# A two-layer state-space and gating kernel: five products a chunk instead of six in most weight tiles

## The reference, cut to what matters

```
def _layer(x, mod, h0, lw, rows):
    shift, scale, gate = jnp.split(mod, 3, axis=-1)
    h = rms_norm(x, norm_w) * (1 + scale[:, None]) + shift[:, None]
    proj = h @ w_in
    xbc_raw, z_m, dt_raw, u_raw, v_raw, z_g, gl_m, gl_g = jnp.split(proj, ...)
    y_m, h_fin = _ssd_branch(xbc_raw, dt_raw, z_m, ...)   # conv of 5 taps, scan in both directions
    y_g = _gmlp_branch(u_raw, v_raw, z_g, ...)
    merged = jax.nn.sigmoid(gl_m) * (y_m @ w_out_m) + jax.nn.sigmoid(gl_g) * (y_g @ w_out_g)
    return x + gate[:, None] * (merged @ w_out), h_fin
```

## Time and profile before

| | |
|---|---|
| median of 3 runs | 1404.17 us (1403.57 to 1405.57) |
| span of the profiled execution, first to last instruction | 1402.5 us |
| TensorE busy | 1389.5 us, 10045 products |
| VectorE busy | 1020.4 us |
| GpSimd busy | 1028.4 us |
| ScalarE busy | 467.2 us |
| HBM read, written | 178.70 MB, 26.02 MB |
| mean granted TensorE clock | 0.997 |

### The profile page before, as it was taken

One profiled execution on the slowest core, in us unless ns is written; L12 is line 12 of the kernel. 1 busy time (PEld: TensorE's weight loads), 2 busy tenths in 40 slices (PEclk: granted clock), 3 DMA queues, 4 the chain that ended last, 5 costly groups with the idle time before them and its releaser, 6 DMA issues.

```text
span 1402.5 us, 26918 instructions
## 1 busy us (share of the span) xinstructions
PE 1389.5 (99%) x10045; PEld 1333.8 (95%) x10045; DVE 1020.4 (73%) x1503; ACT 467.2 (33%) x1040; POOL 1028.4 (73%) x1421
## 2 busy tenths in 40 slices
PE   8999999999999999999999999999999999999997
PEld 6899899999999999999998999999999999999997
DVE  4888679675677688989978766986566776769234
ACT  4432133213766333001242323241266661320122
POOL 3699886596654589998869898757765546979773
PEclk9999999999999999999999999999999999999999
DMA  9262665223766555444334455732346655453222
GB/s 369 91 151 86 184 164 165 68 61 121 186 187 183 170 222 210 149 154 149 110 136 122 106 164 148 179 99 61 106 132 190 192 177 190 149 189 121 76 76 90
DMA packets 197902, 206.31 MB, mean 147 GB/s; under 512 B 76576, under 2 KB 163744, under 8 KB 196640
## 3 DMA queue, kind: packets, MB, share of 16 engines
q1 hardware_dynamic: 115856, 154.61, 35.4%
q10 hardware_dynamic: 81936, 50.16, 12.2%
HBM read 178.70 MB, written 26.02 MB: 146 GB/s over the span
## 4 chain that ended last, share of the span: by engine, by line
PE 98%; DVE 1%; issue 0%; POOL 0%; ACT 0%; DVEq 0%; POOLq 0%; ACTq 0%
PE acc L708 80%; PE X L675 5%; PE acc L675 3%; PE X L947 2%; PE X L927 2%; PE X L963 1%; PE X L988 1%; PE acc L841 1%; PE X L956 1%; PE acc L788 0%; PE X L800 0%; DVE h_pre L1622 0%; DVE xr L2107 0%; DVE p_lo L1577 0%; PE acc L800 0%
## 5 line engine op out<-in xcount | busy, mean ns | idle before, releaser
L609 POOL CAST w_hi<-w_st 128x256 fp32r<-128x256 f32 x696 | 412.7, 607 | 340.8 <-PE acc L708 168.7
L613 POOL TENSOR_TENSOR w_lo<-w_st,w_hi 128x256 fp32r<-128x256 f32 x696 | 644.4, 935 | 0.0
L708 PE MATMUL acc<-h_hi,w_hi 128*128 128x320 f32 x1696 | 402.1, 318 | 0.0
L708 PE MATMUL acc<-h_lo,w_hi 128*128 128x320 f32 x1696 | 386.4, 309 | 0.0
L708 PE MATMUL acc<-h_hi,w_lo 128*128 128x320 f32 x1696 | 386.1, 309 | 0.0
L708 PEld LDWEIGHTS acc<-h_hi,w_hi 128*128 128x128 f32 x1696 | 284.5, 188 | 14.7 <-issue 11.8
L708 PEld LDWEIGHTS acc<-h_hi,w_lo 128*128 128x128 f32 x1696 | 283.5, 188 | 0.0
L708 PEld LDWEIGHTS acc<-h_lo,w_hi 128*128 128x128 f32 x1696 | 283.2, 188 | 0.0
L1788 DVE SCALAR_TENSOR_TENSOR cv<-raw,convw_sb,cv 128x642 f32<-128x642 f32 x128 | 137.1, 1071 | 4.5
L1511 DVE SCALAR_TENSOR_TENSOR ada_acc<-ada_st,sc,ada_acc 128x512 f32<-128x512 f32 x112 | 107.1, 995 | 1.8
L1251 ACT ACTIVATE cvt<-cv 128x642 f32<-128x642 f32 x32 | 23.8, 744 | 162.6 <-DVE cv L1788 162.6
(11 more groups left out here) (266 smaller groups left out, 2320.9 us busy)
## 6 DMA issues: line engine op xcount, KB each, us to landing
w_st<-in_wts SPq DMA_DIRECT2D x174, 512.0 KB, 3.7
cum_bc<-cum_dram ACTq DMA_DIRECT2D x80, 256.0 KB, 4.9
ada_st<-in_wada SPq DMA_DIRECT2D x34, 512.0 KB, 4.5
ex_bc<-ex_dram ACTq DMA_DIRECT2D x64, 128.0 KB, 3.0
ada_pre<-in_wada SPq DMA_DIRECT2D x14, 512.0 KB, 8.9
xs<-xs_dram SPq DMA_DIRECT2D x64, 80.0 KB, 3.9
mga_dram<-c_buf SPq DMA_DIRECT2D x16, 320.0 KB, 5.7
xf<-xf_dram SPq DMA_DIRECT2D x4, 1280.0 KB, 7.4
```

Source lines behind the costliest of these rows:

```text
L609: nc.gpsimd.tensor_copy(quarter(w_hi, slot, q), quarter(w_st, slot, q)).then_inc(s_pool, 1)
L613: nc.gpsimd.tensor_tensor(quarter(w_lo, slot, q), quarter(w_st, slot, q), f(quarter(w_hi, slot, q)), ALU.subtract).then_inc(w_split, 1)
L708: last = mm(a[:, hf, 0:n1], w[:, s, cols], x[:, k, hf * HALF:hf * HALF + n1], start=(k == 0 and n == 0), stop=(k == KC - 1 and n == 2))
```

## The change

The tokens of a joined tile are split 384 and 256 (`WIDE`, `NARROW`) instead of 320 and 320. The first bank of the accumulator takes the three products of the first 384 tokens. For the last 256 tokens, w_hi is multiplied with upper and lower rows in one product of 512 columns, which fills the second bank with two halves, and w_lo with the upper rows adds to the first half. The sum of the two halves is taken outside TensorE. For this the upper and lower rows of each operand are placed so that one access pattern reads both (`pair`).

A tile is joined if the rule in `joins` says so. In 114 of the joined tiles (all but those of `T_OUT`) VectorE adds the halves with one reduction (`join`), into the place of the last 256 tokens of the tile's result, and counts `acc_joined` up; ScalarE then takes its function in two pieces (`taken`), the second after that count, from SBUF. In the `T_OUT` tiles VectorE adds the two halves to the residual one after the other.

```diff
+WIDE = 3 * P
+NARROW = TOK - WIDE
+def joins():
+    return [t for t in range(DEPTH * NT) if t % NT >= RAWT and t % NT not in V_AT and t < DEPTH * NT - 2 and (t >= NT or t % NT < T_ZM)]
+JOINED = joins()
+JOIN_AT = {t: n for n, t in enumerate([t for t in JOINED if t % NT < T_OUT])}
...
+    out += [(8 * (T_UZ + n + 1) - 0.1, "join", n) for n in range(16)]
+    out += [(8 * (T_G + 2 * j + 1) - 0.1, "join_glg", j) for j in range(8)]
...
+        def wide_chunk(t, k, hi, lo, pair, ready=None):
+            s, cols = t % 2, slice(k * P, (k + 1) * P)
+            split_in(t, k)
+            a, b = wide(t), acc_of(t)[:, 1, :]
+            both = pair[:, :, k * TOK + WIDE:(k + 1) * TOK]
...
+            mm(a, w_hi[:, s, cols], hi[:, k, 0:WIDE], start=(k == 0), stop=False)
+            mm(a, w_lo[:, s, cols], hi[:, k, 0:WIDE], start=False, stop=False)
+            if k > 0:
+                mm(b[:, 0:NARROW], w_lo[:, s, cols], hi[:, k, WIDE:TOK], start=False, stop=False)
...
+            mm(a, w_hi[:, s, cols], lo[:, k, 0:WIDE], start=False, stop=(k == KC - 1))
+            last = mm(b.rearrange("p (s n) -> p s n", s=2), w_hi[:, s, cols], both, start=(k == 0), stop=(k == KC - 1))
+            if k == 0:
+                last = mm(b[:, 0:NARROW], w_lo[:, s, cols], hi[:, k, WIDE:TOK], start=False, stop=False)
...
             for n, k in enumerate(ks):
-                last = chunk(t, k, hi, lo, ready, more)
+                if t in JOINED:
+                    last = wide_chunk(t, k, hi, lo, pair, ready)
+                else:
+                    last = chunk(t, k, hi, lo, ready, more)
...
+        def taken(t, dst, src, *how, **more):
+            if t not in JOINED:
+                return A(halves(dst), acc_of(t)[:, :, 0:HALF], *how, **more)
+            A(dst[:, 0:WIDE], wide(t), *how, **more)
+            joined(act, t)
+            return A(dst[:, WIDE:TOK], src[:, WIDE:TOK], *how, **more)
...
                 act.wait_ge(cv_ready, NCONV * L + i - 1)
-                for dst, src in pieces(acc_of(t), *raw_row(i), L):
-                    last = A(dst, src, ACT.Copy)
-                free(t, last)
+                ctx_row, lat_row = raw_row(i)
+                A(ctx_row, wide(t)[:, 0:CTX], ACT.Copy)
+                joined(act, t)
+                free(t, A(grid_rows(lat_row, L)[:, 0:NW, :],
+                          wide(t)[:, CTX:WIDE].rearrange("p (r w) -> p r w", w=GW), ACT.Copy))
...
-                        free(t, A(halves(uz[:, n // 2, :]), acc_of(t)[:, :, 0:HALF], ACT.Gelu_apprx_tanh))
+                        free(t, taken(t, uz[:, n // 2, :], uz[:, n // 2, :], ACT.Gelu_apprx_tanh))
...
+            def join(p, dst):
+                t = T0 + p
+                if t in JOIN_AT:
+                    dve.wait_ge(tile_done, t + 1)
+                    both = acc_of(t)[:, 1, :].rearrange("p (s n) -> p n s", s=2)
+                    if len(dst.shape) == 3:
+                        both = both.rearrange("p (r w) s -> p r w s", w=GW)
+                    nc.vector.tensor_reduce(dst, both, AXX, ALU.add).then_inc(acc_joined, 1)
+            def gated(t, dst):
...
+                joined(dve, t)
+                own.mark(STT(out=dst[:, WIDE:TOK], in0=c_buf[0][:, WIDE:TOK], scalar=1.0, in1=dst[:, WIDE:TOK],
+                             op0=ALU.add, op1=ALU.mult))
+                return STT(out=dst[:, 0:WIDE], in0=c_buf[0][:, 0:WIDE], scalar=1.0, in1=wide(t), op0=ALU.add, op1=ALU.mult)
+            def conv_join(i):
+                join(CONV_AT[i], grid_rows(raw_row(i)[1], L)[:, NW:GH, :])
...
                 else:
+                    if L > 0 or i > NRAW:
+                        conv_join(i)
                     evacuated(dve, T0 + CONV_AT[i])
+                    joined(dve, T0 + CONV_AT[i])
...
+                if L == 0 and i == NRAW - 1:
+                    conv_join(NRAW)
                 dve.wait_ge(cvt_ready, NCONV * L + i + 1)
...
                 later(p)
+                if j > 1:
+                    own.wait()
+                    evacuated(dve, T0 + OM_AT[j - 2])
+                    join(GLM_AT[j], c_buf[j % 2][:, WIDE:TOK])
                 evacuated(dve, T0 + GLM_AT[j])
+                if j == 0:
+                    dve.wait_ge(ymhi_ready, 8 * (L + 1))
+                    join(GLM_AT[1], c_buf[1][:, WIDE:TOK])
...
-                ins = TT(halves(mg[:, j, :]), halves(g), acc_of(t)[:, :, 0:HALF], ALU.mult)
+                if t in JOINED:
+                    join(OM_AT[j], mg[:, j, WIDE:TOK])
+                    joined(dve, t)
+                    own.mark(TT(mg[:, j, WIDE:TOK], g[:, WIDE:TOK], mg[:, j, WIDE:TOK], ALU.mult))
+                    ins = TT(mg[:, j, 0:WIDE], g[:, 0:WIDE], wide(t), ALU.mult)
```

More of the change, by code:

```diff
@@ L225, in build, with pair, part_of @@
     ACTB = KC * TOK * 4
+    def pair(name, first, second):
+        return place(name, [P, 2, (second - first) // 4], first, F32R)
+    def part_of(both, i):
+        return both[:, i, 0:KC * TOK].rearrange("p (k n) -> p k n", k=KC)
     r_h = region(ACTB)
-    h_hi = place("h_hi", [P, KC, TOK], r_h, F32R)
     r_hl = region(ACTB)
-    h_lo = place("h_lo", [P, KC, TOK], r_hl, F32R)
+    h_pair = pair("h_pair", r_h, r_hl)
+    h_hi, h_lo = part_of(h_pair, 0), part_of(h_pair, 1)
     h_pre = place("h_pre", [P, KC, TOK], r_hl)
@@ L1027, in _ @@
                 raw_rows = p < RAWT
-                rows, more = ((p_hi, p_lo), 2) if raw_rows else (h, 0)
+                rows, more = ((p_hi, p_lo, None), 2) if raw_rows else (h, 0)
                 ready = (hhi_ready, h_ready, L) if RAWT <= p < RAWT + 3 else None
@@ L1951, in _ @@
                     dve.wait_ge(zt_ready, 16 * L + j + 1)
-                    free(t, STT(out=halves(c_buf[1]), in0=halves(c_buf[0]), scalar=1.0,
-                                in1=acc_of(t)[:, :, 0:HALF], op0=ALU.add, op1=ALU.mult))
+                    free(t, gated(t, c_buf[1][:, :]))
+                    own.wait()
                     evacuated(dve, t)
@@ L1969, in _ @@
                         dve.wait_ge(mga_out[n % 2], 16 * (KC // 2 * L + n // 2))
-                    free(t, STT(out=halves(c_buf[(1, 4)[n % 2]]), in0=halves(c_buf[0]), scalar=1.0,
-                                in1=acc_of(t)[:, :, 0:HALF], op0=ALU.add, op1=ALU.mult))
+                    dst = c_buf[(1, 4)[n % 2]][:, :]
+                    join(T_G + 2 * n + 1, dst[:, WIDE:TOK])
+                    free(t, gated(t, dst))
+                    own.wait()
                 else:
@@ L1998, in _ @@
                 n = 8 * L + j
[L1999 removed]
+                if t not in JOINED:
+                    dve.wait_ge(zt_ready, 16 * L + 8 + j + 1)
                 if j > 0:
@@ L2004, in _ @@
                     dve.wait_ge(mga_out[0], 16 * KC // 2 * (L + 1))
-                free(t, STT(out=halves(c_buf[1]), in0=halves(c_buf[0]), scalar=1.0,
-                            in1=acc_of(t)[:, :, 0:HALF], op0=ALU.add, op1=ALU.mult))
+                if t in JOINED:
+                    join(T_ZM + j, c_buf[1][:, WIDE:TOK])
+                    dve.wait_ge(zt_ready, 16 * L + 8 + j + 1)
+                free(t, gated(t, c_buf[1][:, :]))
+                own.wait()
                 y = xf[:, j, :]
```

86 lines of the change are left out of this document (60 added, 26 removed).

## The result

| kernel | median us | range, runs | profiled span | mean granted clock |
|---|---|---|---|---|
| before | 1404.45 | 1403.57 to 1405.57, 4 | 1402.5 | 0.997 |
| changed | 1438.20 | 1435.50 to 1439.42, 4 | 1437.7 | 0.989 |

The ratio is 1.0239, with a 95% interval of [1.0227, 1.0251]: the change costs 33.8 us. The forecast of 1422.2 us had the sign and the places right, but the time lies above the range of 1403 to 1434.

What follows compares the result with a forecast made beforehand. TensorE, busy 99% of the span, was taken as the bound. Terms -13.4 + 4.4 + 7.4 + 2.3 + 8.6 + 4.9 + 0.4 + 3.4 = +18.0 us gave span 1420.5, time 1422.2 us, range 1403 to 1434.

Steps and rivals of the forecast that it cites:

- The saving of five products: TensorE, joined tiles: five products a chunk instead of six save one fixed part of 13.3 to 14.0 ns, -13.4 us.
- the second: Rival, TensorE's products: fixed cost is paid by columns; 2.4 us or less saved, stands stay, 1433 us; chance 5%.
- The upper bound of the saving: TensorE, joined tiles: 16 us saved if the last tiles' 384s carry 1 ns each that h operands do not.
- The join: VectorE: each of 114 reductions of 512 PSUM values to 256 takes 0.69 us, bounds 0.5 and 1.2.
- Stands of the convolutions: Tiles 12 and 14, both layers: TensorE waits for accumulators freed late, 4.4 us in layer 0, 2.3 in layer 1.
- State products of tile 25: Start of state products: TensorE waits for ScalarE's states copy behind join 0, 7.4 us in layer 0, 8.6 in layer 1.
- the order alone: Start of state products, layer 0: with no lag from the convolutions TensorE would still stand about 3.5 us, the lower bound.
- Tile 70: Gates of layer 1: tile 68's join comes late behind VectorE's adaLN sums, so TensorE stands 4.9 us.
- Tile 39: Both layers: later ScalarE and the split take up the room before tile 41, 0.4 us together.
- Elsewhere: Tiles 26 to 38, 40 to 63, 72 to 85: joins cost nothing, up to 2 us if cover is thinner.
- The clock: TensorE: lower granted clock after each of the two long stands, 1.7 us each, 3.4 us (0 to 8).
- main step: VectorE's order matters, making TensorE wait; wrong if TensorE's waits stay under 10 us in total.

Runs made afterwards that it cites:

- the run of widths: Kernel before plus 160 unread products inside tile 173, sixteen each of widths from 64 to 512 columns, with fresh or the same weights: 1427.63 us (one run).

## Why the prediction was wrong

*The saving of five products, -13.4 us: this is the step that failed.* The prediction had a fixed cost for each product; the runs show a cost that goes with the columns. The saving measured -1.4 us by itself, some -2 within the changed kernel. The fault is in how the rows were read. Each width showed 12 to 14 ns above N/2.4, and I called that a fixed part. But 256 columns had 12.0, 512 had 14.0, and the value tiles, where two of three products in a row use the same weights, were the wrong witness for 512: 227.3 ns, where the 512s of the changed chunk take 231 to 236 and the run of widths has 233.1 with fresh weights, 225 to 232 with the same. On the line 0.452 ns a column the excess is 10.9 ns at 256, 13.2 at 320 and 20.0 at 512. Three widths close to each other and one product of another kind could not tell a constant from a tenth; I had the same numbers for both and gave the second 5%. Its time was 1433 us; with 5.8 us more for the clock, as measured, it would be 1438.8, against 1438.2. The upper bound of the saving was also added up wrongly: 1 ns less for each of the three 384s makes 865 ns a chunk and 14.4 us, not 16.

The rule of the Trainium skill that I set aside there (TensorE: Matmul & The Clock Gate, "Back-to-back issue gap") made the saving 2.4 us, near the measured one; its durations are too short here, as said.

*The join*: predicted 0.69 us; all 114 took 0.64 to 0.70.

*Stands of the convolutions*: predicted 2.8 and 1.6 in layer 0 (4.4), 0.4 and 1.9 in layer 1 (2.3). Measured 1.63 and 2.31 (3.9), 0.79 and 2.56 (3.4). Right in place, cause and total.

*State products of tile 25*: predicted 7.4 and 8.6, measured 4.89 and 5.84. The chain was the predicted one, link by link, but shorter: from conv 15's start to join 0 VectorE took 9.05 us, not the 10.3 of the earlier trace rows, where the last operand's row is 0.7 us long and not 1.42; the lag against TensorE was some 2.7 us, not 3.55; and TensorE didn't come 0.4 us early. The 3.5 us that I put down to the order alone are the 3.38 and 3.70 of the run without the convolutions' joins.

*Tile 70*: predicted 4.9, measured 5.43. *Tile 39*: predicted 0.4, no stand. *Elsewhere*: predicted 0 to 2, measured 2.0, in tiles 8, 27, 29 and 58.

All stands: 28.0 predicted, 25.5 measured.

*The clock*: predicted 3.4 us for two falls, measured 9.2 for five. The mechanism was right and the size wrong twice over. Stands of 2.31 and 2.56 us were enough, so tile 14 counted too, as did tile 70. And behind the two long ones the slow stretch was 6.8 us, twice that in the opening. The opening was a weak witness besides: of the 14 profiles of this case 7 show the fall there and 7 do not, and TensorE's wait before it was 0.61 to 1.25 us in the ones and 0.67 to 0.87 in the others.

The step sum put right: +18.0 + 11.4 (saving) + 5.8 (clock) - 2.5 (stands) + 2.5 (around the stands) = +35.2 us, the span's growth. Neither the saving nor the clock alone would have taken the time out of the range: 1422.2 + 11.4 is 1433.6, 1422.2 + 5.8 is 1428.0, and both together are over it. That the stands' total came out within 10% owes something to errors that cancel, those of tile 25 being 5.3 us too long and the rest 2.8 us too short.

What I said would prove the main step wrong, stands of less than 10 us in all, did not happen. What I said would show the saving, seven tiles in 48.4 to 48.7 us, failed at once, with 49.18.

## What to carry to other kernels

Before counting on fewer, wider products, fit the time over widths that lie far apart and use the same kind of operand: here it was a rate and a floor, and merging products above the floor gave next to nothing. When a second engine is let in to free a buffer, follow that engine's program order up to the point, and then what is queued behind the waiting instruction on the third: the joins cost 0.7 us each and nothing in most tiles, and 35 us where VectorE had a run without idle before them. Price a stand of the matmul engine at its length plus the clock behind it, 1.4 to 2.9 us here behind all but one of the stands over 2 us.
